# Other slots for the attention steps of three mixers in a transformer kernel with split-fp32 matmuls

## What is computed

```python
# first block: layer 0 convolution, layer 1 dilated attention, each followed by a gated feed-forward (swiglu)
logits = einsum("bnidhc,bnjdhc->bndhij", qb, kk) * HEAD_DIM ** -0.5 + bias      # 12 heads in 3 groups
o, lse = softmax-weighted values, log of the denominator
alpha = softmax(stack(lses), axis=0)                                            # over the 3 groups
o = concatenate([outs[g] * alpha[g][..., None] for g in range(3)]) @ w_o

# second block: layer 0 "even" mixer, layer 1 "odd" mixer, each followed by a swiglu
ya = (p[:, :, 0] - lam * p[:, :, 1]) @ v          # 4 heads of two soft-maxes each, then an RMS norm
score = sum_h relu(iq_h . ik) * iw_h              # an index of 8 heads
sel = top_k(score, 64)                            # each query then sees only its 64 best keys
yb = softmax(q . k[sel] ...) @ v[sel]             # 8 heads, one shared key and value
odd: softmax over a window of 128 keys with a sink logit, 16 heads, 4 key and value heads
```

## Time and profile before

| | |
|---|---|
| median of 3 executions | 1296.39 us |
| lowest, highest | 1286.68, 4060.37 us |
| the profiled execution | 1290.6 us, its span 1289.3 us |
| mean granted TensorE clock | 0.980 |

### The profile page before, as it was taken

One profiled execution on the slowest core, in us unless ns is written; L12 is line 12 of the kernel. 1 busy time (PEld: TensorE's weight loads), 2 busy tenths in 40 slices (PEclk: granted clock), 3 DMA queues, 4 the chain that ended last, 5 costly groups with the idle time before them and its releaser, 6 DMA issues.

```text
span 1289.3 us, 24812 instructions
## 1 busy us (share of the span) xinstructions
PE 1209.2 (94%) x9924; PEld 1147.5 (89%) x9924; DVE 929.5 (72%) x1754; ACT 658.7 (51%) x1145; POOL 73.9 (6%) x82
## 2 busy tenths in 40 slices
PE   6998999999998999999978879999999878999999
PEld 6868999999987999999967768999989767999999
DVE  7527698878686888878786658888885556766652
ACT  6326554454446554445555655444444766544441
POOL 2001000001000100003000011000010112000000
PEclk9998999999999999999998989999999989999999
DMA  7852688778753678787533226887775423556561
GB/s 286 236 153 83 217 304 261 250 259 281 249 177 120 212 262 261 237 279 267 195 120 105 99 86 188 269 260 256 257 268 186 135 91 111 184 181 181 182 194 66
DMA packets 81414, 258.10 MB, mean 200 GB/s; under 512 B 9032, under 2 KB 22164, under 8 KB 81300
## 3 DMA queue, kind: packets, MB, share of 16 engines
q1 hardware_dynamic: 75540, 250.69, 59.4%
q10 hardware_dynamic: 5760, 5.83, 1.8%
HBM read 253.82 MB, written 2.67 MB: 199 GB/s over the span
## 4 chain that ended last, share of the span: by engine, by line
PE 74%; DVE 14%; ACT 6%; issue 3%; DMA 2%; POOL 1%; ACTq 0%; SPq 0%; DVEq 0%; POOLq 0%
PE ps L529 66%; DVE wlo L1249 4%; PE ps L580 2%; DVE HL L1255 2%; DVE aacc L1255 1%; DVE X L1255 1%; ACT oS L854 1%; DMA raw<-wall 1%; ACT HH L854 1%; ACT eS L854 1%; PE ps L631 1%; ACT tmp L854 1%; PE ps L627 1%; PE ps L635 1%; PE ps L626 1%
## 5 line engine op out<-in xcount | busy, mean ns | idle before, releaser
L529 PE MATMUL ps<-HH,whi 128*128 128x256 f32 (+1 forms) x2152 | 624.8, 290 | 21.0 <-DVE wlo L1249 7.7
L529 PE MATMUL ps<-HH,wlo 128*128 128x256 f32 (+1 forms) x2152 | 614.2, 285 | 0.0
L529 PE MATMUL ps<-HL,whi 128*128 128x256 f32 (+1 forms) x2152 | 613.7, 285 | 0.0
L854 ACT ACTIVATE whi<-raw 128x1024 fp32r<-128x1024 f32 (+1 forms) x364 | 382.8, 1055 | 355.3 <-PE ps L529 350.4
L1249 DVE TENSOR_TENSOR wlo<-raw,whi 128x1024 fp32r<-128x1024 f32 (+1 forms) x364 | 442.6, 1220 | 50.3 <-ACT whi L854 49.3
L529 PEld LDWEIGHTS ps<-HH,whi 128*128 128x128 f32 x2152 | 414.4, 193 | 39.0 <-issue 25.6
L529 PEld LDWEIGHTS ps<-HL,whi 128*128 128x128 f32 x2152 | 414.6, 193 | 0.5
L529 PEld LDWEIGHTS ps<-HH,wlo 128*128 128x128 f32 x2152 | 414.0, 192 | 0.0
L529 PE MATMUL ps<-GH,whi 128*128 128x256 f32 x704 | 197.6, 281 | 0.6 <-DVE bcol L1453 0.5
L529 PE MATMUL ps<-GL,whi 128*128 128x256 f32 x704 | 197.0, 280 | 0.0
L529 PE MATMUL ps<-GH,wlo 128*128 128x256 f32 x704 | 197.0, 280 | 0.0
(11 more groups left out here) (207 smaller groups left out, 938.6 us busy)
## 6 DMA issues: line engine op xcount, KB each, us to landing
raw<-wall SPq DMA_DIRECT2D x363, 512.0 KB, 4.3
araw<-ada SPq DMA_DIRECT2D x96, 512.0 KB, 4.8
UR<-uscr ACTq DMA_DIRECT2D x32, 142.0 KB, 4.3
oBB<-kbias SPq DMA_DIRECT2D x16, 192.0 KB, 2.5
aTB<-scratch SPq DMA_DIRECT2D x12, 128.0 KB
uscr<-U ACTq DMA_DIRECT2D x8, 143.5 KB, 4.3
out<-X SPq DMA_DIRECT2D x8, 128.0 KB, 2.9
aTB<-scratch SPq DMA_DIRECT2D x12, 64.0 KB
```

The lines of the kernel that those rows point to most:

```text
L529: ins = pe.e.matmul(o, l, r, start=(kt == p.order[0] and i == 0), stop=(kt == p.order[-1] and i == 2))
L854: ac.then_inc(ac.e.activation(o, i, func, **kw), sem)
```

## The change

Only the numbers in the four tables differ. The helpers are gone, and the tables are written out. Each step keeps its instructions, waits and DMAs; In the even mixer 33 of 67 steps stand in another slot, 30 of them later, mostly by one; in the odd mixer 27 of 49, of which 19 are earlier (`score` 0, 2 and 3 with their `exp` and `fact`, most of `turn` 0 to 7) and 8 later (`weigh` 0, 2, 6 and 7, `turn` 12 to 15). Within a slot some follow in another order. In the dilated mixer `score` 1 comes one tile earlier, `turn` 1 one tile later, `share` 2 one tile earlier, `exp` 3 one tile later, and at the start of `outd` `weigh` 3 stands behind `weigh` 2. The DMAs that the tables place (bias tiles of the dilated mixer) move with `score` 1: the six loads for hs 3 are issued right behind those for hs 2.

```diff
-AFTER_D = {6: [("score", 0)], 7: [("score", 1), ("exp", 0)], 8: [("log", 0), ("exp", 1)], 9: [("share", 0), ("log", 1)],
-           10: [("turn", 0), ("share", 1)], 11: [("turn", 1)], 12: [("score", 2), ("score", 3)],
-           14: [("exp", 2), ("exp", 3), ("log", 2)], 16: [("weigh", 0), ("share", 2), ("log", 3)]}
-BEFORE_D = {0: [("weigh", 1), ("turn", 2), ("share", 3)], 4: [("turn", 3), ("weigh", 2)], 1: [("weigh", 3)]}
...
-AFTER_E = by_slot(
-    [(3, "const", 0), (13, "gain", 0)] + [(13 + k, "index", k) for k in range(4)] + [(17 + k, "top", k) for k in range(8)]
-    + [(25, "pick", 0)] + differ(0, 20, 24) + sparse(0, 26) + differ(1, 30, 34) + sparse(1, 32) + differ(2, 38, 46)
-    + sparse(2, 40, 4, 8) + differ(3, 44, 49) + sparse(3, 46))
-AFTER_O = by_slot(
-    [(3, "const", 0)] + attend(0, 8) + attend(1, 10) + attend(2, 12) + attend(3, 16) + attend(4, 20, (4, 5), 7)
-    + attend(5, 22) + attend(6, 24, (3, 4), 5) + attend(7, 26, (3, 3), 4))
+AFTER_D = {
+    6: [("score", 0), ("score", 1)], 7: [("exp", 0)], 8: [("log", 0), ("exp", 1)],
+    9: [("share", 0), ("log", 1)], 10: [("turn", 0), ("share", 1)],
+    12: [("turn", 1), ("score", 2), ("score", 3)], 14: [("exp", 2), ("log", 2), ("share", 2)],
+    16: [("exp", 3), ("weigh", 0), ("log", 3), ("weigh", 1), ("turn", 2)]}
+BEFORE_D = {
+    0: [("share", 3)], 4: [("turn", 3), ("weigh", 2), ("weigh", 3)]}
...
+AFTER_E = {
...
+    28: [("sexp", 0), ("sscore", 0)], 29: [("sfact", 0)], 30: [("dscore", 1)], 31: [("sturn", 0), ("dexp", 1)],
+    32: [("sturn", 1), ("dfact", 1)], 33: [("dturn", 1), ("sscore", 1)], 34: [("sweigh", 0), ("sexp", 1)],
+    35: [("dweigh", 1), ("sfact", 1)], 36: [("dnorm", 1)], 37: [("dout", 1), ("sturn", 2)],
...
+    45: [("sturn", 5), ("dscore", 3)], 46: [("sweigh", 2), ("dfact", 3), ("dexp", 3), ("sscore", 3)],
+    47: [("dweigh", 2), ("dturn", 3)], 48: [("dnorm", 2), ("sexp", 3)],
...
+AFTER_O = {
...
+    14: [("turn", 2)], 15: [("weigh", 0), ("turn", 3), ("turn", 4), ("score", 3)],
+    16: [("weigh", 1), ("turn", 5), ("exp", 3)], 17: [("fact", 3)], 19: [("turn", 6)],
+    20: [("weigh", 2), ("turn", 7), ("exp", 4), ("score", 4)], 21: [("weigh", 3)],
```

## The result

The changed kernel takes 1268.8 us in the median of four executions (1266.0 to 1272.9), the kernel before 1294.7 us; the ratio is 0.983, with a 95% interval of 0.9805 to 0.9856. One of the four executions of the kernel before took 4060 us: the median of 1294.7 counts it, the ratio leaves it out. The forecast was 1270. The profiled execution took 1269.65 us, its span 1268.3 us against 1289.3, so 21.0 us are to be found in the two traces.

The account below looks back on a forecast made before the run. PE was taken as the bound, with 47 us of holes in the three mixers and a lowered clock there. The terms summed to -26, less 3 and 3 deducted, given as -20.5 on 1290.6: 1270 us, 8-in-10 range 1257 to 1285.

Parts of the forecast that it names:

- the plain sum of -26: All three mixers: even -16, odd -9, dilated -1 us, before the deductions for long waits and missed waits.
- The signs named in advance: Observations said to show the forecast right, such as about 18 us without PE work in the even mixer.
- If one of the two new waits comes with half of that stretch, 2 us more are won: Even mixer, first dense head: less of the 0.50 clock seen over 675 to 685 us; part of a -3 term.
- the 1.1 us for the waits of the first head: Even mixer, `dturn` 0 and `dweigh` 0: passed slot 1.5 us less 0.4, part of a -3 term.
- slots 26 to 31: Even mixer: `sscore` 0 asked in slot 28 instead of 26, so `dscore` 1 comes earlier; -2 us.
- Slots 32 to 35: Even mixer: `taken` ahead of `sscore` 1 on DVE, a slot more cover for `dweigh` 1; -4 us.
- Slots 36 to 46: Even mixer: `sweigh` 2 and a later `dscore` 3 cover waits; -7 us, a third of it from clock.
- Term -9: Odd mixer: earlier `exp` and `fact` shorten waits at the turns, scores and weighs; -9 us.
- Term -1: Dilated mixer: `turn` 1 no longer waits for `rcol`, `weigh` 3 waits less for `HL`; -1 us.
- Waits only change places: Rival, chance 0.20: DVE's queue sets the pace of slots 17 to 26; half the sum, 1278 to 1282 us.
- the bound of 6.7 us: POOL's products in `fact`: if all 12 steps take the long form, up to 6.7 us come back.
- The slower rival through slots 41 and 46: Even mixer, chance 0.03: crowded steps hold DVE, PE runs out of banks and the clock falls; 1317 us.

Follow-up runs that it names:

- E3: The kernel before with the new tables of the dilated mixer alone; 1291.5 us, ratio 0.9996.
- E8: The changed kernel with the first dense head's steps and the `top` steps of the even mixer set back as before; 1268.3 us, ratio 0.9813.
- E9: E5 with `dweigh` 0 of the even mixer moved from slot 25 to 26, `dnorm` 0 to 27, `dout` 0 to 28; 1267.4 us, ratio 0.9801.
- E7: The changed kernel with `sscore` 1 back in slot 32, `sexp` 1 and `sfact` 1 a slot earlier; 1272.5 us, ratio 0.9843.
- E12: E5 with the even mixer's steps of dense heads and sparse pairs 2 and 3 back in their old slots; 1273.1 us, ratio 0.9866.
- E4: The kernel before with the new even and odd tables, dilated tables old; 1267.8 us, ratio 0.9804.
- E11: E5 with `score` 0, 2 and 6 of the odd mixer one slot later, their `exp` unmoved; 1270.2 us, ratio 0.9826.
- E1: The kernel before with the new table of the even mixer alone; 1276.5 us, ratio 0.9865.
- E5: The changed kernel with `turn` 1 of the dilated mixer back behind tile 11; 1266.8 us, ratio 0.9805.
- E6: E5 with `score` 1 of the dilated mixer also back behind tile 7; 1265.6 us, ratio 0.9794.
- E10: E5 with `dturn` 2 moved from slot 42 to 43 and `sfact` 3 ahead of `dout` 2 in slot 49; 1272.6 us, ratio 0.9839.
- E2: The kernel before with the new table of the odd mixer alone; 1281.6 us, ratio 0.9907.

## Why the prediction was right, and where it was not

**The whole.** 1270 against 1268.8, and -20.5 against -21.0 in the profiled executions. (-26 with 3 and 3 taken off is -20; half a microsecond of the -20.5 has no term.) But 1.9 of the 21.0 lie ahead of the dilated mixer and between it and the even one, where the change does nothing. The first of these stretches took 343.5 to 346.8 us in the fourteen traces, the second 254.0 or, with a fall of the clock such as the kernel before had, 255.0: these 1.9 us are luck. The change itself gave 19.1. Against the plain sum of -26, 2.6 us are missing in the even mixer, 2.7 in the dilated one and 0.4 in the odd one, and 1.2 came back behind the even mixer: 6.9 in all, where the prediction had taken off 6. It took them off for long waits, the clock behind them and waits missed, mostly in the even and odd mixers; that the allowance was of the right size is in good part luck, as 2.7 of it went to a mixer that it did not think of. The signs named in advance did come: PE without work for 16.4 us in the even mixer (18 said), a clock of 0.93 there (0.93 or more), no long wait of line 635 for `eV`, the one for `eP` at `dweigh` 0, and waits for POOL in the odd mixer of 0.8 us (under 2.5).

**Even mixer, points.** PE's timeline in the changed kernel, against the points of the reckoning (its first score stands at 665.64, 0.2 earlier than before, so the times can be compared directly):

```profile
675.37 0.55 PE L620 MATMUL ps<-ident,eS 128*128 128x128 f32 x3 [0.52 <-DVE eS L1244]
680.98 1.22 PE L624 MATMUL ps<-eP,eV 128*128 128x256 f32 x2 [3.61 <-ACT eP L843]
694.10 0.50 PE L615 MATMUL ps<-eQK 64*128 64x128 f32 x4 [0.82 <-DVE eQK L1244]
702.62 0.52 PE L620 MATMUL ps<-ident,eS 128*128 128x128 f32 x3 [1.55 <-DVE eS L1244]
...
729.37 0.55 PE L620 MATMUL ps<-ident,eS 128*128 128x128 f32 x3 [2.42 <-DVE eS L1244]
740.45 0.59 PE L624 MATMUL ps<-eP,eV 128*128 128x256 f32 x2
742.25 0.55 PE L620 MATMUL ps<-ident,eS 128*128 128x128 f32 x3 [0.98 <-DVE eS L1244]
...
750.82 0.52 PE L620 MATMUL ps<-ident,eS 128*128 128x128 f32 x3 [2.19 <-POOL eS L1748]
754.94 0.98 PE L624 MATMUL ps<-eP,eV 128*64 128x256 f32 x4
```

`dturn` 0 was put at 675.5 and stands at 675.37. `dweigh` 0: 681.2 with a wait of 3.9, and 680.98 with 3.61. `dscore` 1: 693.9 and 694.10. `dweigh` 1: 707.3 and 709.88, the largest miss; the wait of 1.55 us ahead of `dturn` 1 was not in the reckoning, and 3.4 us of half clock lie ahead of it (704.4 to 707.8). The long stall of ACT for `bcol` is down from 6.01 to 2.87 us. `dturn` 2 waits 2.42 (2.3 reckoned), `dweigh` 2 stands at 740.45 (738.5), `dturn` 3 waits 0.98 (1.1), `sturn` 7 2.19 (2.8); `dnorm` 3 doesn't wait (1.3). `sweigh` 3: 753.1 and 754.94. So the last point is 1.8 us late.

**Even mixer, terms.** Up to the scores of dense head 2 the changed kernel wins 8.6 us (60.1 to 51.5 behind the first score), the reckoning -3, -2 and -4. The first two made -5 up to the scores of dense head 1, and 4.5 came. "If one of the two new waits comes with half of that stretch, 2 us more are won" is borne out by E3 (2.1 us between 10.3 and 6.8 us of half clock with the same old table). What failed is the 1.1 us for the waits of the first head: E8 and E9 show that it has no such gain, and slots 26 to 31 hold 2.4 instead of 2. Slots 32 to 35 held their term (27.2 to 23.0 us up to `dscore` 2, 4.1 for 4, with the clock in it), and E7 gives all of it back. Slots 36 to 46 gave 5.1 instead of 7, with 5.7 in E12. "A third of it from clock" was too low: the even mixer has 13.6 us less of half clock than before. That is the table's doing: 23.9 to 27.3 us of half clock in the three traces with the old even table, 6.8 to 13.7 in the six with the changed one. What it is worth depends on where the falls lie. The changed table took 88.3 us with 6.8 of half clock (E4, E11), 88.7 with 12.8 (E1), 89.6 with 10.2 (E5, E6) and 90.2 with 13.7 (the changed kernel), the old one 102.0 with 23.9 and 103.6 with 27.3: between 0.08 and 0.48 us lost for each us. So, as an estimate, 1 to 7 of the 13.4 us are clock; the runs don't fix it closer. By the row, the 0.50 over the whole of 675 to 685 is 0.83 there now.

Not foreseen is that the gain is given back in part: in the stretch behind the even mixer the clock fell for 3.4 us, +1.2, in the changed kernel as in E1, E4, E8, E11 and E12, and for 6.8 in E10; in E5, E6, E7 and E9, without a fall, this stretch is as short as before (235.2 to 235.3). No trace with the old even table has such a fall (before, E2, E3); what brings it stays open.

**Odd mixer.** Term -9, measured -8.1 and 0.5 more behind it; alone (E2) -7.2. Measured from a projection common to both (997.71 before, 985.95 now), 11.8 us are to be taken off the points: `turn` 6 1024.1 reckoned, `score` 6 1039.6, `weigh` 7 1056.8, its k-block 1058.7; PE's timeline has them 0.7 to 1.5 us later:

```profile
1025.61 0.55 PE L620 MATMUL ps<-ident,oS 128*128 128x128 f32 x3 [0.76 <-POOL oS L1748]
...
1040.31 0.50 PE L615 MATMUL ps<-oK,oQ 64*128 64x128 f32 x4 [1.67 <-DVE oQ L1244]
...
1057.53 0.66 PE L624 MATMUL ps<-oP,oV 128*64 128x256 f32 x4
...
1059.36 0.39 PE L518 MATMUL ps<-HH,whi 128*128 128x256 f32 x1 [0.95 <-DVE HL L1238]
```

and the views of waits went from POOL 5.2, `oQ` 4.2, `oP` 2.8 to the following, where the matmuls that weigh no longer wait for `oP` at all and the transpositions wait 2.2 (2.8 before):

```profile
PE ps L615 <- DVE oQ L1244: 4.7, 3, 1.8
PE ps L620 <- ACT oP L843: 2.2, 4, 0.7
...
PE ps L620 <- POOL oS L1748: 0.8, 1, 0.8
```

**Dilated mixer.** Term -1, measured +1.7. The failed step is the whole term's silence on the clock: each move was priced by its wait, and `turn` 1 put ahead of the two scores was booked as "no longer waits for `rcol`, -0.4". The waits did what was said (`aP` 2.2 to 0.9, `HL` 1.5 to 2.4, the copy for `turn` 2 earlier; -1.0 in E5), but 6.8 to 10.2 us of half clock took 2.4 to 4.4 us (65.5 us in E3 and E8, 67.6 in E10, against 63.1 in E5). "The dilated mixer longer than 66.5 us would show that `aV` behind `weigh` 1 is the dearer place" was a wrong test too: it was longer, at 67.0, and E5 has the same place of `aV` at 63.1.

**Rivals and bounds.** "Waits only change places" is right as a mechanism for slots 20 to 27, and for E10 and E11; it is wrong for the rest. The products of POOL take the long form in 6 of 12 `fact` steps as before, now split 3 and 3 over the mixers, so the bound of 6.7 us was not touched. POOL's timeline, the first two of the odd mixer:

```profile
998.94 1.61 POOL L1748 TENSOR_TENSOR oS<-oS,oST 128x256 f32<-128x256 f32 x2 [28.75 <-DVE oST L1713]
1006.71 2.50 POOL L1748 TENSOR_TENSOR oS<-oS,oST 128x256 f32<-128x256 f32 x2 [6.16 <-DVE oST L1713]
```

DVE worked on `wlo` beside each of the long ones, and beside none of the short ones, in both traces. The rule of the Trainium skill ("SBUF — State Buffer", "SBUF: two separate sides") that was drawn on agrees with this, but only says what a meeting costs and not how many there will be. The slower rival through slots 41 and 46 didn't come: DVE waits 0.35 us ahead of `sfact` 2 and 1.30 ahead of `dfact` 3.

## What to carry over

A wait of one slot in an engine's order is won only where the engine that it waits for has room: look first whether that engine's rows have gaps in the stretch, because otherwise each move (E8, E9) only picks the place of the wait. A move that lets another engine's routine work (here the emptying of a bank) go first can be worth more than one that lets PE ask later, since two or three queues hang on it (E7, 4.0 us with the clock; `dweigh` 0 asked later, E9, nothing). And count what a move does to PE's mix of work: thin steps set side by side can cost more in granted clock than the wait that they save (`turn` 1: 0.4 us saved).

## What was not expected of the hardware

The granted clock fell while PE was never idle for over 0.35 us: 7.5 us of transpositions and 64-row scores in a row brought 6.8 us of half clock in 4 of 4 traces, 5.3 us of scores in 2 of 10. The Trainium skill ("TensorE: Matmul & The Clock Gate", the table in "Why this matters for your kernels") warns of idle gaps between bursts of matmuls; the falls here are not of that kind. Two executions of the same table can differ by 4.4 us in 67 through this alone (E5 and E10, dilated mixer), which is as much as the best single move was worth (4.0 us, E7). So a difference of this size is judged by traces cut at the same instructions and held against others with as much half clock, and not by one total.
